# Mask, sink and softmax of the causal attention's 32 steps, spread over four engines

## The reference, cut to what matters

```python
s = einsum('bnqkgd,bnskd->bnkgqs', q, kb) * 64 ** -0.5       # 128 queries x 256 keys
valid = (k_pos >= 0) & (k_pos <= q_pos) & (q_pos - k_pos < 128)
s = where(valid, s, -1e30)
p = softmax(concatenate([s, sink], axis=-1), axis=-1)[..., :-1]
o = einsum('bnkgqs,bnskd->bnqkgd', p, vb)
return o @ w_o + b_o
```

## Time and profile before

| | |
|---|---|
| median of 3 runs | 3258.42 us (3256.18 to 3265.27) |
| the profiled execution, its own time | 3261.72 us |
| its span in the trace | 3259.9 us |
| busy: PE, PEld, DVE, ACT, POOL | 94%, 75%, 33%, 29%, 35% |
| the stage `attention(1)` | about 2711 to 2807.5 us, 3% of the span |

### The profile page before, as it was taken

One profiled execution on the slowest core, in us unless ns is written; L12 is line 12 of the kernel. 1 busy time (PEld: TensorE's weight loads), 2 busy tenths in 40 slices (PEclk: granted clock), 3 DMA queues, 4 the chain that ended last, 5 costly groups with the idle time before them and its releaser, 6 DMA issues.

```text
span 3259.9 us, 48776 instructions
## 1 busy us (share of the span) xinstructions
PE 3054.4 (94%) x20648; PEld 2430.7 (75%) x20648; DVE 1088.8 (33%) x1489; ACT 958.1 (29%) x1191; POOL 1153.3 (35%) x317
## 2 busy tenths in 40 slices
PE   8979999999999967999997999998999997899999
PEld 6748778887888845778994688886888865678886
DVE  4451242223211265234444421116211156541212
ACT  3153232223222246322212322223222235531222
POOL 4304334343443432322210343444344341234334
PEclk9989999999999978999997999999999999999999
DMA  4202222222222212331101122222222220122222
GB/s 182 89 3 92 95 85 91 103 91 87 94 91 102 90 52 116 133 114 36 43 14 40 65 97 97 91 92 89 90 90 91 93 90 27 40 78 92 95 97 78
DMA packets 41560, 271.76 MB, mean 83 GB/s; under 512 B 4624, under 2 KB 4752, under 8 KB 11568
## 3 DMA queue, kind: packets, MB, share of 16 engines
q1 hardware_dynamic: 38304, 252.60, 22.0%
q10 hardware_dynamic: 3088, 16.65, 1.3%
HBM read 254.55 MB, written 14.68 MB: 83 GB/s over the span
## 4 chain that ended last, share of the span: by engine, by line
issue 63%; PE 16%; POOL 16%; DVE 4%; DVEq 1%; POOLq 0%; ACT 0%; DMA 0%; ACTq 0%
POOL w_lo L434 15%; PE ps L701 6%; PE ps L529 3%; PE ps L531 2%; PE ps L530 2%; PE ps L616 1%; DVE small L1467 1%; POOL x_res L497 1%; DVEq L1466 0%; DVE work L1326 0%; PE ps L623 0%; DVE work L1409 0%; DVE ybuf L1482 0%; DVEq L1406 0%; DVE x_res L1407 0%
## 5 line engine op out<-in xcount | busy, mean ns | idle before, releaser
L434 POOL TENSOR_TENSOR w_lo<-w_raw,w_hi 128x2048 fp32r<-128x2048 f32 x220 | 1024.5, 4657 | 1834.7 <-ACT w_hi L910 1825.5
L529 PE MATMUL ps<-act_hi,w_hi 128*128 128x512 f32 x2304 | 920.7, 400 | 47.0 <-DVE act_lo L1354 24.4
L530 PE MATMUL ps<-act_lo,w_hi 128*128 128x512 f32 x2304 | 914.2, 397 | 0.0
L531 PE MATMUL ps<-act_hi,w_lo 128*128 128x512 f32 x2304 | 913.8, 397 | 0.0
L910 ACT CAST w_hi<-w_raw 128x2048 fp32r<-128x2048 f32 x219 | 417.4, 1906 | 1038.9 <-PE ps L531 1014.8
L529 PEld LDWEIGHTS ps<-act_hi,w_hi 128*128 128x128 f32 x2304 | 437.0, 190 | 165.2 <-POOL w_lo L434 30.4
L530 PEld LDWEIGHTS ps<-act_lo,w_hi 128*128 128x128 f32 x2304 | 437.2, 190 | 102.8 <-issue 1.7
L531 PEld LDWEIGHTS ps<-act_hi,w_lo 128*128 128x128 f32 x2304 | 436.8, 190 | 102.9
L529 PE MATMUL ps<-hid_hi,w_hi 128*128 128x512 f32 x1120 | 444.2, 397 | 10.2 <-POOL w_lo L434 7.9
L531 PE MATMUL ps<-hid_hi,w_lo 128*128 128x512 f32 x1120 | 442.7, 395 | 0.0
L530 PE MATMUL ps<-hid_lo,w_hi 128*128 128x512 f32 x1120 | 442.5, 395 | 0.0
(11 more groups left out here) (254 smaller groups left out, 2393.8 us busy)
## 6 DMA issues: line engine op xcount, KB each, us to landing
w_raw<-stream SPq DMA_DIRECT2D x224, 1024.0 KB, 4.8
spill<-work ACTq DMA_DIRECT2D x5, 2048.0 KB, 6.3
scratch<-spill SPq DMA_DIRECT2D x24, 256.0 KB, 3.3
work<-bias_in SPq DMA_DIRECT2D x1, 3072.0 KB, 19.0
x_res<-x_in SPq DMA_DIRECT2D x2, 1024.0 KB, 8.2
spill<-area ACTq DMA_DIRECT2D x4, 512.0 KB, 4.9
work<-spill SPq DMA_DIRECT2D x1, 2048.0 KB, 8.6
area<-spill SPq DMA_DIRECT2D x7, 256.0 KB, 2.8
```

The source lines that it names most:

```text
L434: tt(w_lo[:, s, :], w_raw[:, s, :], w_hi[:, s, :].bitcast(F32), ALU.subtract).then_inc(S["lo_made"], 1)
L529: mm(out, wh, hi[:, k, :], start=(k == 0), stop=False)
L530: mm(out, wh, lo[:, k, :], start=False, stop=False)
L531: return mm(out, wl, hi[:, k, :], start=False, stop=end)
```

## The change

The mask and the sink move from VectorE to TensorE. Ahead of the steps VectorE copies the two masks and an identity matrix as fp32r into `hid_hi` (before the slabs of `q2` are read out). In a step each head first gets a matmul of the identity with one column of sinks, which puts the sink into column 256 of the score bank; then, for each of the two key blocks, a matmul of identity and mask opens the accumulation (`start=True, stop=False`) and the score matmul adds to it. VectorE takes the maximum over 257 columns straight from PSUM, and ScalarE the exponential of 257 columns straight from PSUM, so that the sum holds the sink already. GpSimd scales the rows, VectorE copies the outputs that ScalarE copied before, and TensorE's loop runs one step deeper: S(t), T(t-3), O(t-4). `p1_buf` has four buffers, and O alternates between banks 3 and 5.

```diff
@@ VectorE, ahead of the q2 slabs
+            dve.wait_ge(S["swa_loaded"], 16)
+            copy(mask_r, swa_mask.rearrange("p (b k) -> p b k", b=2))
+            copy(ident_r, c("ident")).then_inc(S["sw_mask"], 1)
@@ GpSimd
+            def softmax():
+
+                for t in range(STEPS[1]):
+                    pool.wait_ge(S["sw_recip"], t + 1)
+                    for h in range(2):
+                        p = p1_buf[:, t % 4, h, 0:256]
+                        inst = nc.gpsimd.tensor_scalar(p, p, tiny(RECIP, t, 4)[:, h:h + 1], None, ALU.mult)
+                    inst.then_inc(S["sw_p"], 1)
...
+                if name == "mixer1_post":
+                    split(done, FIRST["o2"] + 1)
+                    softmax()
+                    done = FIRST["o2"] + 1
@@ TensorE
+            def attention_1():
+
+                steps = STEPS[1]
+                for t in range(steps + 4):
+                    if t == 3:
+                        pe.wait_ge(banks_free[1], FIRST["o2"] // 2)
+                    if t < steps:
+                        if t >= 2:
+                            pe.wait_ge(S["sw_exp"], t - 1)
+                        for h in range(2):
+                            out = ps[:, SCORE_BANKS[t % 2] + h, :]
+                            mm(out[:, 256:257], c("ident"), sinks[:, 2 * (t // 4) + h:2 * (t // 4) + h + 1], start=True, stop=True)
+                            for part, keys in enumerate(swa_k(t, h)):
+                                half = out[:, 128 * part:128 * part + 128]
+                                mm(half, ident_r, mask_r[:, min(t % 4, 1), 128 * part:128 * part + 128], start=True, stop=False)
+                                inst = mm(half, swa_q(t, h), keys, start=False, stop=True)
+                        inst.then_inc(S["sw_s"], 1)
+                        if t < 4:
+                            stay_warm(1, bank=5)
+                    if 3 <= t <= steps + 2:
+                        u = t - 3
+                        pe.wait_ge(S["sw_p"], u + 1)
...
+                                inst = nc.tensor.transpose(ps[:, TURN_BANKS[u % 2], 256 * h + 128 * part:256 * h + 128 * part + 128],
+                                                           p1_buf[:, u % 4, h, 128 * part:128 * part + 128], c("ident"))
+                        inst.then_inc(S["sw_pt"], 1)
+                    if t >= 4:
+                        u = t - 4
+                        pe.wait_ge(S["sw_ptsb"], u + 1)
+                        if u >= 2:
+                            pe.wait_ge(S["sw_osb"], u - 1)
...
@@ ScalarE
+                for t in range(steps + 3):
+                    if t < steps:
+                        act.wait_ge(S["sw_max"], t + 1)
+                        if t >= 2:
+                            act.wait_ge(S["sw_recip"], t - 1)
+                        if t >= 4:
+                            act.wait_ge(S["sw_pt"], t - 3)
+                        for h in range(2):
+                            inst = af(p1_buf[:, t % 4, h, :], ps[:, SCORE_BANKS[t % 2] + h, 0:257], ACT.Exp,
+                                      bias=tiny(NEG_MAX, t)[:, h:h + 1], accum_out=tiny(SUM, t)[:, h:h + 1])
+                        inst.then_inc(S["sw_exp"], 1)
+                    if t >= 3:
+                        u = t - 3
+                        act.wait_ge(S["sw_pt"], u + 1)
...
@@ VectorE
+                for t in range(steps + 5):
+                    if t < steps:
+                        dve.wait_ge(S["sw_s"], t + 1)
+                        nc.vector.tensor_reduce(tiny(MAX, t), ps[:, SCORE_BANKS[t % 2]:SCORE_BANKS[t % 2] + 2, 0:257], AX_X, ALU.max)
+                        dve.drain()
+                        if t >= 2:
+                            dve.wait_ge(S["sw_exp"], t - 1)
+                        ts(tiny(NEG_MAX, t), tiny(MAX, t), -1.0, None, ALU.mult).then_inc(S["sw_max"], 1)
+                    if 1 <= t <= steps:
+                        u = t - 1
+                        dve.wait_ge(S["sw_exp"], u + 1)
...
+                        nc.vector.reciprocal(tiny(RECIP, u, 4), tiny(SUM, u)).then_inc(S["sw_recip"], 1)
+                    if t >= 5:
+                        u = t - 5
+                        dve.wait_ge(S["sw_o"], u + 1)
+                        copy(work[:, u // 4, 128 * (u % 4):128 * (u % 4) + 128], ps[:, 3 + 2 * (u % 2), 0:128]).then_inc(S["sw_osb"], 1)
```

More of the change, by code:

```diff
@@ L242, in build, with tiny @@
         pt_buf = yflat[:, 3072:4096].rearrange("p (b h a k) -> p b h a k", b=2, h=2, a=2)
+        p1_buf = yflat[:, 0:2056].rearrange("p (b h k) -> p b h k", b=4, h=2)
+        pt1_buf = yflat[:, 2056:3080].rearrange("p (b h a k) -> p b h a k", b=2, h=2, a=2)
+        swa_mask = work[:, 18, :]
+        mask_r, ident_r = hid_hi[:, 0, :].rearrange("p (b k) -> p b k", b=2), hid_hi[:, 1, 0:128]
+        NEG_MAX, SUM, MAX, RECIP = 12, 16, 20, 24
+        def tiny(at, t, count=2):
+            return small[:, at + 2 * (t % count):at + 2 * (t % count) + 2]
         vb_buf = scratch[:, 2, :].rearrange("p (b k) -> p b k", b=2)
@@ L795, in _ @@
                 pe.wait_ge(banks_free[s], 6)
-            attention(0, na_q, na_k, None)
+            attention(0, na_q, na_k)
             pe.wait_ge(S["at_osb"], STEPS[0])
@@ L894, in _ @@
             pe.wait_ge(S["vtok_out"], 1)
-            attention(1, swa_q, swa_k, swa_v)
+            pe.wait_ge(S["sw_mask"], 1)
+            attention_1()
             post_slabs("mixer1_post", FIRST["o2"], act_hi, act_lo,
@@ L1085, in attention, with attention_1 @@
                         nc.scalar.copy(work[:, tile, 128 * j:128 * j + 128], ps[:, 3, 0:128]).then_inc(S["at_osb"], 1)
+            def attention_1():
+                steps = STEPS[1]
+                for t in range(steps + 3):
[5 more added lines that the diff above has]
+                            act.wait_ge(S["sw_pt"], t - 3)
+                        for h in range(2):
+                            inst = af(p1_buf[:, t % 4, h, :], ps[:, SCORE_BANKS[t % 2] + h, 0:257], ACT.Exp,
[4 more added lines that the diff above has]
+                        act.wait_ge(S["sw_pt"], u + 1)
+                        if u >= 2:
+                            act.wait_ge(S["sw_o"], u - 1)
+                        nc.scalar.copy(pt1_buf[:, u % 2, :, :, :],
+                                       ps[:, TURN_BANKS[u % 2], :].rearrange("p (h a k) -> p h a k", h=2, a=2)).then_inc(S["sw_ptsb"], 1)
             def mix(j, wait):
@@ L1292, in _ @@
             root("mixer1_pre")
[L1293 removed]
+            act.dma_start(swa_mask.rearrange("p (b k) -> p b k", b=2), swa_in).then_inc(S["swa_loaded"], 16)
             for n in range(1, 4):
@@ L1793, in _ @@
                     tt(q, q, b.unsqueeze(2).broadcast_to([P, 2, T]), ALU.add).then_inc(banks_free[s], 1)
-            dve.wait_ge(S["swa_loaded"], 16)
-            swa_mask = work[:, 18, :].rearrange("p (b k) -> p b k", b=2)
-            attention(1, lambda t: swa_mask[:, min(t % 4, 1), :].unsqueeze(1).broadcast_to([P, 2, 256]))
+            attention_1()
             for k in range(NT):
```

39 lines of the change are left out of this document (19 added, 20 removed).

## The result

The change makes the kernel slower: 3401.51 us (3398.95 to 3408.97, 4 runs) against 3258.24, a ratio of 1.0433, 95% interval 1.0413 to 1.0453, or +143 us. I had forecast +36.

A forecast was written before the change was run, and what follows sets the result against it. VectorE bounds the attention stage at 2.84 us a step; afterwards TensorE would, at 2.77 + 0.59 + 0.62 = 3.98 us. That gives +35.6 us on the median 3258.42, so 3294 us, range 3280 to 3316.

The forecast's parts named there:

- VectorE is the bound before, and TensorE after.: Attention stage: VectorE sets the step of 2.84 us before; TensorE's queue sets 3.98 us after.
- A change of shape costs 0.20 us, ten of them a step.: TensorE's queue: each change of matmul shape costs 0.20 us, with ten a step instead of three.
- S at 2.77 us.: TensorE's score group for both heads, sinks and masks included, in one step: 2.77 us against 0.65 before.
- the score: One score matmul alone between two shape changes: overlapping loads 0.11, columns and emptying 0.20, sum 0.32 us.
- my own path: Attention stage: S(4) at 2726.1, then 27 steps of 3.98 us, then 9.5 us to the first cast; +35.6 us.
- TensorE falls to half its clock in the stage (8%): Rival, 8%: half clock makes a step 6.6 us; 3306 if for 30 us, 3375 if for the whole stage.
- the factor of the half clock: Attention stage at half clock: T takes 0.97 us against 0.59, 1.65 times as long.
- GpSimd 0.73 us for a row of 256: GpSimd's scaling in a step: 0.73 us for one of 256 columns, 1.5 us for both.
- The two copies ahead of `q2`, about 1 us and hidden.: VectorE's new copies ahead of `q2`: about 1 us, hidden by the second read-out's wait of 2.02 us for TensorE.
- The Trainium skill's drain at a change of tiling mode: TensorE: changing the tiling mode, and not merely the tile, drains the engine; 0.17 us of idle in the trace.

The follow-up runs named there:

- run 9: The change without its TensorE part: VectorE adds the mask into SBUF, GpSimd writes sinks and scales, deeper loop kept, ScalarE's copy ahead of the exponentials; 3231.03 us, ratio 0.9914.
- Run 8: The kernel before with only the scaling of the rows moved to GpSimd, in the loop as it was; 3274.73 us, ratio 1.0036.
- run 5: The kernel before plus four idle one-column matmuls a step, one ahead of each score matmul; 3391.76 us, one execution.
- run 6: The kernel before plus four idle one-column matmuls a step, standing together ahead of the four score matmuls; 3291.13 us, one execution.
- run 7: The change ordered within each head: sink, one mask matmul of 256 columns, then two scores; 3294.41 and 3364.69 us in two executions.
- run 3: The change plus two warm-up matmuls of 128x512 in each step, ahead of the products with the values; 3386.21 us, one execution.
- run 1: The change ordered by shape: both heads' sinks and masks (one mask matmul of 256 columns each) first, then the four scores; 3255.83 us, ratio 0.9986.

## Why the prediction was wrong

- **VectorE is the bound before, and TensorE after.** Right, and so is that the gains elsewhere meet no need: the waits above, and run 9, which takes just those gains. Run 8 adds that the scaling alone does not pay in the loop of before; the deeper loop was not tested by itself.
- **A change of shape costs 0.20 us, ten of them a step.** Right: the change's first head has sink and mask at the forecast 0.22 and 0.26, and behind a score's second load the next one comes 0.31 us later, against 0.11 within it. Runs 5 and 6 show with nothing else changed that the order costs time at one clock too: both at half, a step is 7.04 against 5.06 us.
- **S at 2.77 us.** Too low. It measured 3.14 at full clock. The term that was mis-sized is the score: I took its two passes to overlap and had 0.32, but what overlaps are the two heads (run 7); alone it is 0.42. Four of them, 0.4 us a step. With 3.14 + 0.59 + 0.62 = 4.35 us a step (4.34 in run 3) my own path gives S(4) 1.5 us later, 27 steps of 0.37 more, 10 us, and 0.4 behind them: about +48 us instead of +36, or 3306, inside the range.
- **"TensorE falls to half its clock in the stage (8%)".** This is the step that failed. It happened, for 235 of the stage's 242 us. My argument against it was that the stage before holds full clock with matmuls busy for 13.81 of 20 us, and that the new one has fewer pauses. It has fewer, and lost the clock all the same: 40 of 40 us are busy at half. The busy time misled, since the ends of PE rows are modelled: the two passes of a sink, of one column each, are listed as 0.59 us above. The earlier trace rows already had the higher busy share at the half clock. What my argument left out is that the same scores, transposes and products were to be spread over half as long a step again, with ten changes of shape between them. Measured cost: S, T and O at half are 5.37, 1.05 and 1.05, 7.47 us a step, where I had 6.6 for this rival. Of the 0.9 us between, some 0.6 are S's price and 0.3 the factor of the half clock: 7.47 against 4.35 is 1.72, and I took 1.65 from the T of the earlier trace rows, whose 0.97 us begin 0.16 us before the clock fell. The stage grew from 96 to 242 us: some 98 of the 146 are the clock (32 steps of 3.1), and some 48 the longer step at full clock.
- **GpSimd 0.73 us for a row of 256.** Too low: 0.92. It was hidden under TensorE's step in the change; in run 9 it is the bound.
- **The two copies ahead of `q2`, about 1 us and hidden.** They took 1.65 us until the next instruction of VectorE, and are hidden all the same: the second read-out behind them (2680.24) still waits for TensorE, and comes 5.71 us behind VectorE's copy of 128x512 ahead of them, at 2674.53; before, it was 5.72 us.

```profile
2675.29 1.59 DVE L1882 CAST hid_hi<-work 128x512 fp32r<-128x512 f32 x1
2676.80 0.21 DVE L1883 CAST hid_hi<-cst 128x128 fp32r<-128x128 f32 x1
...
2680.24 1.22 DVE L1888 SCALAR_TENSOR_TENSOR work<-ps,scratch 128x1024 f32 x1 [0.69 <-PE ps L556]
```

- **The Trainium skill's drain at a change of tiling mode** (TensorEngine Tiling (Array Packing), Key Properties) agrees with the traces read here: some 0.2 us behind each change at full clock. In this kernel what came behind it, the lost clock, was the larger part.

What stays open: which quality of TensorE's work the chip goes by. The traces order the kernels roughly by changes of shape: with three the clock is full but for 3.4 us at the stage's start in the kernel before (the rows below), with four full in run 1 and lost for 48 us in run 6, with six lost for 20 us in run 7, with ten lost to the end of the stage but for one short return in run 5. But the kernels vary the columns for each us with it, run 6 against run 1 and the two executions of run 7 show that the count alone does not decide, and the warm-up matmuls moved the clock without taking a change of shape away. The kernel before:

```profile
2712.00:2719.80 7.80, 5.82 (x35) 2.88 (x36) 6.83 (x21) 4.42 (x18) 0.00 (x0) 1.00 0.00 0
2719.80:2723.20 3.40, 3.40 (x22) 2.51 (x22) 2.48 (x9) 2.50 (x10) 0.00 (x0) 0.50 0.00 0
2723.20:2807.00 83.80, 57.38 (x584) 40.67 (x582) 69.72 (x228) 60.54 (x230) 0.00 (x0) 1.00 0.01 1
```

## What to carry to other kernels

Work that goes to an engine with idle time is priced in its queue order, not in its count: small matmuls of another tile shape between others cost a gap at each change (here 0.20 us), and they also part neighbours that ran side by side. Group matmuls by shape within a step. And read a "busy" TensorE together with its granted clock and the time for one matmul: after a change that breaks up its work, whether the full clock stays is to be checked first; here its loss was 98 of the stage's 242 us.

## What the runs showed of the hardware

- TensorE stood at half clock for 235 us while no other engine held its queue up (the change), and for 201 us in the kernel before with four idle matmuls in alternating places (run 5). In both, matmuls were listed as busy nearly all the time (40.00 of 40 us, 198.98 of 200).
- Adding matmuls of 128x512 to the steps shortened them: 7.47 us with none, 7.2 on average with one and 7.0 with two.
- A change of shape behind an fp32 matmul of 128 columns makes the next load come about 0.20 us later at full clock and 0.35 at half; a score alone takes 0.42 and 0.72 us at the two levels.
- Two scores of one head in a row take 0.52 us of loads, four of two heads on different partitions 0.53.
- A one-operand scaling by a column of factors on GpSimd, 128x256 fp32 in SBUF, took 0.92 us.
